# Hybrid layers: five of the eleven up projection sets as seven products on sums of blocks, in parts of 2, 2, 3 and 4 sets

## What is computed

```python
x = layer_norm(ALPHA * x + mix, ln1_g, ln1_b)
up = causal_dwconv(jnp.einsum('bsd,df->bsf', x, w_up), ffn_conv_w)   # 1024 -> 2 * 2816, three taps along the tokens
a, b = jnp.split(up, 2, axis=-1)
ffn = jnp.einsum('bsf,fd->bsd', jax.nn.silu(a) * b, w_down)          # 2816 -> 1024
return layer_norm(ALPHA * x + ffn, ln2_g, ln2_b)
```

## Time and profile before

| | us |
|---|---|
| median of 3 runs (2874.51 to 2875.99) | 2875.15 |
| the profiled execution | 2874.51 |
| its span, first to last instruction | 2872.4 |
| busy: PE, ScalarE (ACT), VectorE (DVE), GpSimd (POOL) | 2843.7, 1681.7, 1271.4, 407.3 |

### The profile page before, as it was taken

One profiled execution on the slowest core, in us unless ns is written; L12 is line 12 of the kernel. 1 busy time (PEld: TensorE's weight loads), 2 busy tenths in 40 slices (PEclk: granted clock), 3 DMA queues, 4 the chain that ended last, 5 costly groups with the idle time before them and its releaser, 6 DMA issues.

```text
span 2872.4 us, 37827 instructions
## 1 busy us (share of the span) xinstructions
PE 2843.7 (99%) x14218; PEld 2400.4 (84%) x14218; DVE 1271.4 (44%) x2409; ACT 1681.7 (59%) x2449; POOL 407.3 (14%) x472
## 2 busy tenths in 40 slices
PE   9999999999999999999999999999999999999999
PEld 7989889889997778988887887888878788788887
DVE  6654736364444645644336116422254511632235
ACT  7676757566665755655656445544554744554454
POOL 1111111111111001111110111111111011111110
PEclk9999999999999999999999999999999999999999
DMA  9776767788887428888893897788869389778884
GB/s 249 156 157 137 176 139 156 162 191 193 188 190 160 89 62 202 187 186 200 192 193 86 186 194 168 187 190 205 196 163 199 80 193 192 172 189 189 202 191 117
DMA packets 137015, 492.97 MB, mean 172 GB/s; under 512 B 15344, under 2 KB 15600, under 8 KB 136720
## 3 DMA queue, kind: packets, MB, share of 16 engines
q0 software_dynamic: 67296, 239.30, 45.4%
q1 hardware_dynamic: 68688, 249.59, 30.0%
q10 hardware_dynamic: 864, 1.78, 0.2%
HBM read 488.52 MB, written 2.10 MB: 171 GB/s over the span
## 4 chain that ended last, share of the span: by engine, by line
PE 95%; ACT 2%; DVE 2%; DVEq 1%; issue 0%; ACTq 0%
PE ps L1263 68%; PE ps L1423 8%; PE ps L1282 5%; PE ps L1685 3%; PE ps L1382 1%; PE ps L1626 1%; PE ps L1605 1%; PE ps L1832 1%; ACT arena L1134 1%; PE ps L1539 1%; PE ps L1343 0%; PE ps L1365 0%; PE ps L1810 0%; PE ps L1615 0%; DVE XT L2507 0%
## 5 line engine op out<-in xcount | busy, mean ns | idle before, releaser
L511 ACT ACTIVATE wh<-raw 128x1024 fp32r<-128x1024 f32 (+2 forms) x465 | 479.2, 1031 | 813.2 <-PE ps L1263 732.7
L494 POOL DMA_DIRECT2D wl<-weights x465 | 405.4, 872 | 2429.7 <-ACT wl L518 2429.7
L1263 PE MATMUL ps<-HH,wh 128*128 128x512 f32 x1840 | 720.9, 392 | 2.9 <-DVE HL L2515 2.1
L1263 PE MATMUL ps<-HH,wl 128*128 128x512 f32 x1840 | 716.4, 389 | 0.0
L1263 PE MATMUL ps<-HL,wh 128*128 128x512 f32 x1840 | 716.2, 389 | 0.0
L518 ACT ACTIVATE wl<-raw 128x1024 fp32r<-128x1024 f32 (+2 forms) x465 | 473.6, 1018 | 9.1 <-DVE arena L2130 9.1
L1263 PE MATMUL ps<-MH,wh 128*128 128x512 f32 x1056 | 411.8, 390 | 0.7 <-DVE ML L2394 0.7
L1263 PE MATMUL ps<-MH,wl 128*128 128x512 f32 x1056 | 411.0, 389 | 0.0
L1263 PE MATMUL ps<-ML,wh 128*128 128x512 f32 x1056 | 410.9, 389 | 0.0
L1263 PEld LDWEIGHTS ps<-HH,wh 128*128 128x128 f32 x1840 | 345.4, 188 | 78.1 <-issue 3.8
L1263 PEld LDWEIGHTS ps<-HL,wh 128*128 128x128 f32 x1840 | 345.5, 188 | 72.7 <-issue 1.4
(11 more groups left out here) (373 smaller groups left out, 4009.1 us busy)
## 6 DMA issues: line engine op xcount, KB each, us to landing
raw<-weights SPq DMA_DIRECT2D x468, 512.0 KB, 5.1
wl<-weights POOLq DMA_DIRECT2D x417, 512.0 KB, 7.5
wl<-weights POOLq DMA_DIRECT2D x48, 384.0 KB, 6.3
XT<-x SPq DMA_DIRECT2D x4, 512.0 KB, 8.3
out<-XT SPq DMA_DIRECT2D x3, 512.0 KB, 2.7
arena<-tables POOLq DMA_DIRECT2D x1, 1024.0 KB, 10.9
arena<-table_h ACTq DMA_DIRECT2D x1, 640.0 KB, 5.7
arena<-swaps_a POOLq DMA_DIRECT2D x1, 576.0 KB, 8.2
```

The lines of the kernel that those rows point to most:

```text
L494: pool.dma_start(wl[:, n, first:], weights[slab][:, first:], accum_op=ALU.add).then_inc(w_lo[n], 16)
L511: act_f(wh[:, n, at:w], raw[:, n, at:w], ACT.Copy)
L1263: op = mm(bank(g, t), w[:, slot, at:at + P], x[:, first + kt, :], start=(kt == 0 and w is wh and x is xh), stop=(kt == n_k - 1 and w is wl ...
```

## The change

Parts are now 2, 2, 3 and 4 sets; the sets of the second and third part (`H_TWIST`) become 4 and 6 twisted sets. Their results go through taps, silu and product a tile at a time (`up_twisted`), and their `twist_raw`, `twist_high` and `twist_low` are written between. The sums of x that the products need are made in the first part (`up_input_sums`, after its first set; ScalarE's high parts of them after three slabs of its second set). Because they need x itself, the factor ALPHA moves from the end of the layer norm to the first `residual`. `twist_sums` is reordered in all twisted sets (one more drain, two fewer blocks of space). Four memsets move to the start of each hybrid layer, and tiles get other places in the arena. The numbers of slabs, of DMAs and of down projection matmuls stay. Cut to its core:

```diff
-H_PARTS = ((0, 3), (3, 4), (7, 4))
+H_PARTS = ((0, 2), (2, 2), (4, 3), (7, 4))
+H_TWIST = ((2, 2), (4, 3))
...
@@ -1062,13 +1073,70 @@
+            def up_twisted(first, sets):
+                k, g, s, sp = c.take("tw", 2 * sets).n, c.take("group", 2 * sets), c.take("slab", 4 * sets), \
+                    c.take("split", 2 * sets)
+                high_parts(s + 4, 1)
+                twist_copy(k, g, tw_up)
+                high_parts(s + 5, 1)
+                for i in range(2 * sets):
+                    if i < 2 * sets - 2:
+                        twist_high(k + 2 + i)
+                    act.wait_ge(tw_sum, k + i + 1)
+                    for t in range(2):
+                        tap = L_TAPS + 4 * (2 * UP_SETS + first + i // 2) + 2 * t + i % 2
+                        act_f(up_y[:, t, :], up_out[:, t, :], ACT.Identity, scale=lpar[:, tap:tap + 1])\
+                            .then_inc(up_tap, 1)
+                    more = i + 1 < 2 * sets
+                    if more:
+                        high_parts(s + (6 + 2 * i), 1)
+                    act.wait_ge(up_a, k + i - 23)
+                    act_f(up_silu, up_y[:, 0, :], ACT.Silu).then_inc(up_gate, 1)
+                    if more:
+                        twist_copy(k + i + 1, g + (i + 1), tw_up)
+                    write_high(MH[:, i, :], up_hf, sp + i)
+                    if more:
+                        high_parts(s + (7 + 2 * i), 1)
+            def down_before_twist():
+                k = c.at["tw"].n
+                c.take("group")
+                n = c.take("slab", 2)
+                high_parts(n + 4, 2)
+                twist_high(k)
+                c.take("group")
+                n = c.take("slab", 2)
+                high_parts(n + 4, 1)
+                twist_high(k + 1)
+                high_parts(n + 5, 1)
...
+                    if first == 0 and k == sets - 1:
+                        at = 2 * (c.at["tw"].n - 24) // H_SUMS
+                        g, last = set_of(4, lambda: up_sum_highs(at), 3)
+                    else:
+                        g, last = set_of(4, done=0 if first or k else 2)
...
@@ -1081,7 +1149,15 @@
                 set_of(sets)
-                if first != H_PARTS[-1][0]:
+                if first == 0:
+                    twist_high(c.at["tw"].n)
+                    c.take("group")
+                    s = c.take("slab", sets)
+                    high_parts(s + 4, 2)
+                    twist_high(c.at["tw"].n + 1)
+                    if sets > 2:
+                        high_parts(s + 6, sets - 2)
+                elif first != H_PARTS[-1][0]:
                     set_of(sets)
...
@@ -1738,10 +1820,18 @@
             def up_part(first, sets, ready, high_ready=None):
                 s = c.at["split"]
-                for k in range(sets):
-                    features(4, HH, HL, ready, high_ready=None if k else high_ready)
-                    c.take("split", 2)
-                    c.take("up")
+                if (first, sets) in H_TWIST:
+                    at = c.at["tw"].n - 24
+                    if at % (2 * H_SUMS) == 0:
+                        pe.wait_ge(up_done, 4 * (at // (2 * H_SUMS)) + 4)
+                    for i in range(2 * sets):
+                        twist_set(c.take("tw").n, layer_sums)
+                    c.take("split", 2 * sets)
+                else:
+                    for k in range(sets):
+                        features(4, HH, HL, ready, high_ready=None if k else high_ready)
+                        c.take("split", 2)
+                        c.take("up")
                 features(sets, MH, ML, split_ready(s))
                 if first != H_PARTS[-1][0]:
                     features(sets, MH, ML, nothing)
...
@@ -2133,19 +2223,20 @@
...
-                v.tensor_tensor(tw[:, 5:7], tw[:, 4:5].broadcast_to((P, 2, 256)), tw_bank(g, 2), ALU.add)
-                dve.drain()
-                v.tensor_tensor(tw[:, 1:3], tw[:, 5:7], tw_bank(g, 3), ALU.add).then_inc(free, 1)
-                v.tensor_tensor(tw[:, 3], tw[:, 5], tw_bank(g, 2)[:, 1], ALU.add).then_inc(free, 1)
+                v.tensor_tensor(tw[:, 1:3], tw[:, 4:5].broadcast_to((P, 2, 256)), tw_bank(g, 2), ALU.add)
+                dve.drain()
+                v.tensor_tensor(tw[:, 3], tw[:, 1], tw_bank(g, 2)[:, 1], ALU.add).then_inc(free, 1)
+                dve.drain()
+                v.tensor_tensor(tw[:, 1:3], tw[:, 1:3], tw_bank(g, 3), ALU.add).then_inc(free, 1)
                 dve.drain().then_inc(tw_sum, 1)
...
@@ -2548,17 +2635,82 @@
...
+            def up_input_sums(n):
...
+                v.tensor_tensor(s1, x21, x22, ALU.add).then_inc(up_sum, 1)
+                dve.drain()
+                v.tensor_tensor(s2, s1, x11, ALU.subtract).then_inc(up_sum, 1)
+                v.tensor_tensor(s3, x11, x21, ALU.subtract).then_inc(up_sum, 1)
+                dve.drain()
+                v.tensor_tensor(s4, x12, s2, ALU.subtract).then_inc(up_sum, 1)
+                for m in range(4):
+                    dve.wait_ge(up_hi, n + m + 1)
+                    v.tensor_tensor(up_sums[m][1], up_raw[m], up_sums[m][0], ALU.subtract).then_inc(up_done, 1)
+            def up_twisted(first, sets):
+                k, s, sp = c.take("tw", 2 * sets).n, c.at["slab"], c.take("split", 2 * sets)
+                def low_part(i):
+                    dve.wait_ge(split_hi, (sp + i).value(1))
+                    v.tensor_tensor(ML[:, i, :], up_hf, MH[:, i, :], ALU.subtract).then_inc(split_done, 1)
+                for i in range(2 * sets):
+                    twist_sums(k + i, tw_up)
+                    if i:
+                        low_part(i - 1)
+                    if i < 2 * sets - 2:
+                        twist_low(k + 2 + i)
+                    for t in range(2):
+                        dve.wait_ge(up_tap, 2 * (k + i - 24) + t + 1)
+                        for w in (1, 0):
+                            at = L_TAPS + 4 * (w * UP_SETS + first + i // 2) + 2 * t + i % 2
+                            y = up_y[:, t, 2 - w:S]
+                            if not w:
+                                dve.drain()
+                            v.scalar_tensor_tensor(out=y, in0=up_out[:, t, 0:S - 2 + w], scalar=lpar[:, at:at + 1], in1=y,
+                                                   op0=ALU.mult, op1=ALU.add)
+                        done = dve.drain()
+                        if t == 0:
+                            done.then_inc(up_a, 1)
+                    if i < 2 * sets - 3:
+                        twist_raw(k + 3 + i, s + (6 + 2 * i))
+                    dve.wait_ge(up_gate, k + i - 23)
+                    v.tensor_tensor(up_hf, up_silu, up_y[:, 1, :], ALU.mult).then_inc(split_src, 1)
+                low_part(2 * sets - 1)
+            def down_before_twist(sets, scale):
+                k, s = c.at["tw"].n, c.at["slab"] + 2 * sets
+                twist_raw(k, s)
+                residual(sets, 0, scale)
+                twist_low(k)
+                twist_raw(k + 1, s + 2)
+                twist_low(k + 1)
+                residual(sets, 1, scale)
+                twist_raw(k + 2, s + 4)
...
@@ -2579,6 +2731,11 @@
+                    if first == 0 and k == sets - 2:
+                        up_input_sums(2 * (c.at["tw"].n - 24) // H_SUMS)
+                if first == 0:
+                    down_before_twist(sets, ALPHA)
+                    return
                 residual(sets, 0)
```

More of the change, by code:

```diff
@@ L94 @@
 GATE_LEAD = 14
-H_LAYER = dict(slab=120, group=38, split=4 + 8 + 8 + 2 * UP_SETS + 8, att=16, hl=1, sq=16, ln=2, ts=2, up=UP_SETS)
+H_SUMS = sum(sets for _, sets in H_TWIST)
+H_LAYER = dict(slab=120, group=32 + 2 * len(H_PARTS) + H_SUMS, split=4 + 8 + 8 + 2 * UP_SETS + 8, att=16, hl=1, sq=16, ln=2, ts=2,
+               up=UP_SETS - H_SUMS, tw=2 * H_SUMS)
 class Pos:
@@ L786, in ffn @@
             def ffn(between, layer):
-                s0, k0 = c.at["slab"], 12 * layer
+                s0, k0 = c.at["slab"], c.take("tw", 12).n
                 def first_quarter():
@@ new lines, in down_before_twist @@
+            def down_before_twist():
[9 more added lines that the diff above has]
+                high_parts(n + 5, 1)
+            def up_part(first, sets):
+                if (first, sets) in H_TWIST:
+                    up_twisted(first, sets)
+                    if any(first + sets == after for after, _ in H_TWIST):
+                        down_before_twist()
+                    else:
+                        set_of(sets)
+                        set_of(sets)
+                    return
@@ L1066, in up_part @@
                 for k in range(sets):
                     n = c.take("up")
-                    g, last = set_of(4, done=0 if first or k else 2)
+                    if first == 0 and k == sets - 1:
[3 more added lines that the diff above has]
+                        g, last = set_of(4, done=0 if first or k else 2)
                     wait_used(act, last)
                     s = c.take("split", 2)
```

(37 more changed lines are left out.)

68 lines of the change are left out of this document (42 added, 26 removed).

## The result

The changed kernel takes **2906.3 us** (median of 4 runs, 2904.35 to 2909.46) beside 2874.8 us for the kernel before (4 runs, 2874.29 to 2875.99): 1.0108 times as long, 95% interval 1.0096 to 1.0121. The forecast was 2893 us with a range to 2903: the sign and the mechanism held, the size did not.

What follows compares the result with a forecast made beforehand. PE was taken to bound the kernel. Per layer, 10.1 us saved against 17.7 waited, with slower low-half landing, gave 8.2 us lost, 16.4 for both; plus 1.4 for the clock: 2893 us, range 2882 to 2903.

Steps and rivals of the forecast that it cites:

- PE bounds, and any wait put before it is time added: Hybrid networks: PE works without a break, so a removed matmul saves time and a wait before PE adds it.
- Saving 2.02 us a set: Up sets: two twisted sets take 19.74 us against 21.76 for a plain one; 10.1 us saved a layer.
- First part, 5.4 us a layer: Two plain sets: the down projection reaches the last set's tiles too early, so PE waits 5.4 us.
- Second part, 1.3 for weights, 0.3 and 2.6 for tiles: Four twisted sets: PE waits for the fourth set's weights and the third and fourth tiles, 4.2 us a layer.
- Third part, full steps of 14.3 us, waits of 3.7 and 4.4: Six twisted sets: VectorE's steps outlast PE's 9.87 us, delaying the fifth and sixth sets, 8.1 us a layer.
- the clock's term: Half-clock matmuls after PE's stalls: between nothing and 12 us for six stalls, 1.4 us taken for all.
- 2 us a stall: Upper price of half-clock work after one stall, if it lasts as long as the fall took; 12 for six.
- Rival 3: The clock falls at each of the six stalls and the knock-on goes through: 2904 us; chance 12%.
- The lower end of the range: 2882 us: full steps a whole microsecond shorter, 8 us less for both layers, and no fall of the clock.
- Rival 1: Twisted parts: steps fit and matmuls decide; 9.5 us waited against 10.1 gained, 2874 us, no change; chance 5%.
- rival 2: Faster: first-part waits are filled too by a shorter chain; needs waits under 7.2 us a layer; chance 5%.
- Rival 4: The change does not do what it says: a twisted set takes more than 9.87 us; chance 2%.

Runs made afterwards that it cites:

- The two experiments on order: Changed kernel with ScalarE's silu ahead of the low-half write that waits for `twist_raw`: 2901.0 us; changed kernel with `twist_raw` before the taps: 2895.5 us.
- version with PE crossing: Four-set version, PE taking the second half's first down-projection tile ahead of the first half's last tile in twisted parts: 2865.3 us, ratio 0.9965.
- the parts alone: Kernel before, all sets plain, in the change's parts of 2, 2, 3 and 4 sets: 2903.7 us, ratio 1.0101.
- four-set version: Changed kernel with parts of 3, 2, 2 and 4 sets, the middle two twisted, `twist_raw` before the taps: 2871.9 us, ratio 0.9986.
- the same parts in the change's order: Four-set version with `twist_raw` after the taps, as in the change: 2877.6 us, ratio 1.001.
- silu first: Changed kernel with ScalarE's silu ahead of the low-half write that waits for `twist_raw`: 2901.0 us, ratio 1.0082.
- memsets-alone run: Kernel before with only the four memsets moved to the start of each hybrid layer: 2875.6 us, ratio 1.0001.

## Why the prediction was right and wrong

*PE bounds, and any wait put before it is time added*: right. The two experiments on order took away waits, and with them falls of the clock, but no work, and the time followed.

*Saving 2.02 us a set*: right. In the first twisted part of the version with PE crossing, which has no wait, four sets take 1923.56 - 1884.10 = 39.5 us, 9.87 each, against 21.76 for a plain one. (The forecast read the 21.76 between two operations of VectorE and said that both had waited for PE; the earlier trace rows has them wait for ScalarE. The distance is right all the same.) The networks of that version take 331.8 and 330.7 us against 336.5: 4.7 and 5.8 shorter. In the first layer 8.1 saved less 0.9 waited at a tile and 0.95 idle with nothing to wait for leave 6.3; in the second 8.1 less 0.5 at a tile and 0.4 for `twist_low` leave 7.2. So 1.5 us a layer stand in starts behind waits and in small gaps.

*First part, 5.4 us a layer*: measured 4.9 and 5.4 (10.3). Right, and so was its reason: the parts alone show 5.2 a stall.

*Second part, 1.3 for weights, 0.3 and 2.6 for tiles*: measured 1.71, 0.53 and 2.36 in the first layer, 2.15, 0.44 and 2.36 in the second. Right within a microsecond, and at the sets and tiles named. VectorE's `twist_sums` there start at 1869.12, 1882.85, 1893.07 and 1900.97: 13.7, 10.2 and 7.9 apart, forecast 13.6, 10.1 and 7.3.

*Third part, full steps of 14.3 us, waits of 3.7 and 4.4*: steps measured at 14.6 us. The chain in order of time shows one such step whole (start, us, what):

```profile
1947.43 0.85 ACT wl L529
1948.27 0.53 ACT arena L1101
1948.83 0.70 DVE arena L2687
...
1950.92 0.73 ACT wl L529
1951.66 1.81 ACT arena_r L767
1953.50 2.29 DVE arena_r L2224
1955.79 0.66 DVEq L2678
...
1961.31 0.70 DVE arena L2220
1962.04 0.84 ACT wl L529
```

From `wl` to `wl` it is 1962.04 - 1947.43 = 14.6 us: silu and product behind the write that waited, then two halves of a slab, `twist_high`, `twist_low`, the taps and `twist_raw`, in series over two engines. `twist_sums` starts 14.0, 14.6, 14.6, 10.2 and 7.5 us apart. The waits came as 4.1 and 2.1 in the first layer and 5.1 and 2.0 in the second, 6.2 and 7.1 against 8.1. The second of each pair is shorter than the 4.4 told for a reason that the forecast did not have: PE's work between the two ran at half clock for 5.8 us and so came 2.9 us later to a set that started when its weights were there. With these 2.9 us it is 5.0 and 4.9, and the chain is as told. All the waits together are 33.2 us against 35.4, and would be about 39 without a fall.

**The step that failed is the clock's term: 1.4 us was taken. PE lost 16.7 us to half clock in the trace, about 10.9 of them beyond what shortened a wait.** The forecast knew that the clock falls when PE is idle and named its bounds (0 to 12), then took a value near the lower one. Two of its inputs were wrong, and one effect was missing. It drew from the earlier trace rows that the clock falls about 4 us after the last matmul, and made of this a condition that stalls of under 4 us would be spared. Of the twelve waits of the changed kernel eight are followed by a fall: four of 4.1 to 5.4 us, but also two of 2.4 us (at 1910 and 2640 us) and two of 2.0 and 2.1 (at 1984 and 2714), while others of 1.7 and 2.2 (at 1888 and 2618) are not. One reading of the tail says how long that fall took, not how short a gap can do it.

The price, "2 us a stall", was the other input. As a bound it happened to be near the mark (1.6 on average measured in the parts-alone kernel; 1.7 reckoned for a fall of 3.4 us behind a stall, and 2.3 to 2.9 for those of 6.8, which begin inside it). What was missing is that time lost ahead of another wait is not lost twice.

Rival 3, "the clock falls at each of the six stalls", was the case that came about, with eight falls (the end of the second part is among them); it had been given 12% because its condition was read from the tail. Its 12 us for the clock are near the 10.9, by luck in part, since two more falls came than it had and two of the eight cost next to nothing in the end. With 16.7 us in place of 1.4 and the measured waits, the forecast's own sum gives 2875.2 - 20.2 + 33.2 + 16.7 = 2904.9, and the starts behind the waits make it 2906.8. The lower end of the range had a slip that changed nothing: 2891.6 - 8 is 2883.6, and the 2882 comes from 7.6 us a layer, not the 8.2 taken.

The rule that the Trainium skill gives (TensorE: Matmul & The Clock Gate, "HAM oscillation — how this bites in real kernels"), that idle gaps bring the clock to half and the next burst starts cold, agrees with these traces, though not behind every gap: 0.43 us a matmul behind the gap, and 6.3 us back when four gaps were filled. It had stood in the forecast beside the sum and changed nothing in it.

Rival 1 (the steps fit) and rival 2 (faster) needed waits of under 10 us a layer; 16.6 were there. Rival 4 is out: a twisted set takes 9.87 us where nothing is waited for.

## What to carry to other kernels

When a kernel runs at full clock without a gap, a new stall costs its length and may cost a stretch of half-speed matmuls behind it: here 1.6 us on average for a fall, and falls came even behind stalls of 2 us, though not behind each. Put this into the sum from the start, but not where another wait with an end of its own stands right behind, and if a wait can't be removed, a needless matmul in it may pay if it ends before the wait does. Before cheaper products are put in, work out the chain on the other engines for one tile in its written order, since average load (VectorE idle half the time) says nothing of it: first give the last tile of every part its cover, then look for writes that wait ahead of what someone needs sooner.

## What the runs showed of the hardware that was not expected

- The granted clock fell after a wait of 1.96 us (the four-set version, half clock from about 1932.6 to 1936), and in the same execution not after waits of 1.97, 1.61 and 1.59 us. In the same parts in the change's order four waits were 2.34 to 2.38 us, and one was followed by a fall. With silu first, a wait of 3.03 us (at 1967 us) was not. So the length of a wait of 2 to 3 us does not say here whether the clock falls. The falls in the networks lasted 3.4 us or twice that, whatever the length of the stall.
- A fall at 946 to 947 us stands in four of the twelve profiled executions, one of them the memsets-alone run, and not in that of the kernel before. Two executions can differ by 0.9 us by this alone.
- At half clock 128x512 matmuls start 0.43 us apart, the same as twice 0.2265 less some 5%; the weight loads beside them lengthen too (190 to 330 ns at most).
- A needless fp32 matmul with 512 columns took 0.87 us and stands as two records in the trace, against 0.227 for one in fp32r.
